# Additions of the gated branch products move from VectorE to GpSimd in a two-layer hybrid decoder trunk

## What is computed

```
h = RMSNorm(x)
proj = h @ w_in                        # 4 gates of width 1024, and the inputs of the four branches
o_a, o_b, o_c, o_d = gMLP, block-sparse attention, latent attention, convolution    # 256 tokens x 256 each
y = sum over n of sigmoid(gate_n) * (o_n @ w_branch[n])       # 256 x 1024
x = x + y @ w_out
x = x + channel_mixer(RMSNorm(x))
```

## Time and profile before

| | |
|---|---|
| device time, median of 3 | 1124.6 us |
| device time of the profiled execution | 1124.35 us |
| its span | 1122.6 us |
| TensorE busy | 1064.7 us (95%), 5632 matmuls |
| VectorE busy | 838.5 us (75%) |
| ScalarE busy | 646.7 us (58%) |
| GpSimd busy | 29.0 us (3%) |
| chain that ended last | TensorE 74%, VectorE 18%, ScalarE 5% |
| mixer of layer 0, mixer of layer 1 | about 17 to 232 us, about 436 to 650 us |

### The profile page before, as it was taken

The page is one execution under the profiler, slowest core; times in us unless marked ns, Lnnn a source line. Parts: engine busy times, 40 slices in busy tenths (PEclk is TensorE's granted clock), DMA queues, the critical chain, the costliest instruction groups (busy, mean ns, idle before and its releaser), DMA issues.

```text
span 1122.6 us, 15778 instructions
## 1 busy us (share of the span) xinstructions
PE 1064.7 (95%) x5632; PEld 910.9 (81%) x5632; DVE 838.5 (75%) x1178; ACT 646.7 (58%) x904; POOL 29.0 (3%) x76
## 2 busy tenths in 40 slices
PE   5999999999999999999899969999999999999997
PEld 4888777889999998888687857888787878788886
DVE  4579888654545447579898565988889898989895
ACT  4667545443434336456545345666767676667664
POOL 6000000030000000000000000000000000000000
PEclk9999989999999999999999988999999999999999
DMA  9554445675455454444345374899898989898981
GB/s 264 178 169 150 150 132 180 210 205 187 152 187 174 169 195 156 152 160 160 125 155 198 119 258 146 292 326 334 297 342 290 357 286 357 289 350 300 353 296 58
DMA packets 125324, 248.64 MB, mean 221 GB/s; under 512 B 4912, under 2 KB 50034, under 8 KB 125280
## 3 DMA queue, kind: packets, MB, share of 16 engines
q1 hardware_dynamic: 123136, 243.02, 63.4%
q0 software_dynamic: 2144, 5.03, 1.9%
HBM read 246.99 MB, written 1.05 MB: 221 GB/s over the span
## 4 chain that ended last, share of the span: by engine, by line
PE 74%; DVE 18%; ACT 5%; issue 2%; DMA 1%; ACTq 0%; DVEq 0%; POOL 0%; POOLq 0%
PE bank L349 22%; PE bank L351 21%; PE bank L350 21%; DVE wlo L337 8%; ACT whi L330 3%; PE bank L899 2%; PE bank L898 2%; PE bank L957 1%; DVE h L1355 1%; DVE dacc L1560 1%; PE bank L612 1%; DVE x L1353 1%; DVE h L1492 1%; DMA gain<-in_attn_norm 1%; PE bank L919 1%
## 5 line engine op out<-in xcount | busy, mean ns | idle before, releaser
L337 DVE TENSOR_TENSOR wlo<-ring,whi 128x1024 fp32r<-128x1024 f32 (+3 forms) x506 | 541.1, 1120 | 108.3 <-ACT whi L330 107.4
L349 PE MATMUL bank<-whi,hTh 128*128 128x512 f32 (+3 forms) x1328 | 479.3, 361 | 11.4 <-DVE wlo L337 8.8
L330 ACT CAST whi<-ring 128x1024 fp32r<-128x1024 f32 (+3 forms) x506 | 457.1, 972 | 30.1 <-PE bank L351 17.6
L351 PE MATMUL bank<-whi,hTl 128*128 128x512 f32 (+3 forms) x1328 | 469.2, 353 | 0.0
L350 PE MATMUL bank<-wlo,hTh 128*128 128x512 f32 (+3 forms) x1328 | 469.1, 353 | 0.0
L349 PEld LDWEIGHTS bank<-whi,hTh 128*128 128x128 f32 x1328 | 252.4, 190 | 51.6 <-DVE wlo L337 15.7
L351 PEld LDWEIGHTS bank<-whi,hTl 128*128 128x128 f32 x1328 | 252.2, 190 | 30.6
L350 PEld LDWEIGHTS bank<-wlo,hTh 128*128 128x128 f32 x1328 | 252.5, 190 | 28.3 <-issue 0.5
L349 PE MATMUL bank<-whi,oTh 128*128 128x512 f32 x128 | 53.2, 415 | 4.0 <-DVE oTl L1666 4.0
L1678 DVE SCALAR_TENSOR_TENSOR act<-bank,rstd,sig 128x256 f32<-128x256 f32 x22 | 9.6, 479 | 57.9 <-ACT sig L1209 57.9
L350 PE MATMUL bank<-wlo,oTh 128*128 128x512 f32 x128 | 51.7, 404 | 0.0
(11 more groups left out here) (299 smaller groups left out, 877.7 us busy)
## 6 DMA issues: line engine op xcount, KB each, us to landing
ring<-in_w_in SPq DMA_DIRECT2D x40, 1024.0 KB, 5.2
ring<-in_moe_w_down SPq DMA_DIRECT2D x40, 1024.0 KB, 6.0
ring<-in_moe_w_gate SPq DMA_DIRECT2D x32, 1024.0 KB, 7.2
ring<-in_moe_w_up SPq DMA_DIRECT2D x32, 1024.0 KB, 7.3
ring<-in_moe_w_gate SPq DMA_DIRECT2D x16, 768.0 KB, 6.1
ring<-in_moe_w_up SPq DMA_DIRECT2D x16, 768.0 KB, 4.5
ring<-in_ffn_w_gate SPq DMA_DIRECT2D x11, 1024.0 KB, 5.3
ring<-in_ffn_w_up SPq DMA_DIRECT2D x11, 1024.0 KB, 5.4
```

The source lines that it names most:

```text
L330: nc.scalar.copy(whi[pc.part(hf)][:, 0:n], pc.raw[:, hf * n:(hf + 1) * n]).then_inc(hi_done, 1)
L337: nc.vector.tensor_tensor(wlo[q][:, 0:n], pc.raw[:, hf * n:(hf + 1) * n], whi[q][:, 0:n].bitcast(F32), ALU.subtract).then_inc(lo_done, 1)
L349: nc.tensor.matmul(o, sh, wh, start=start, stop=False)
L351: return nc.tensor.matmul(o, sl, wh, start=False, stop=stop)
```

## The change

The products stay on VectorE and now count on a semaphore of their own, `br_used`. The additions of the steps j = 2 to 7 are done by GpSimd in `merged_sums(l)`, two for each step, and they count on `br_ev`. For j = 0 and 1, where there is nothing to add, VectorE waits for its two products and raises `br_ev` by 2 with an empty instruction. `branch(j)` on TensorE waits for the products alone; `gate_ev` and `merged_T` still wait for `br_ev`, now for GpSimd's additions.

```diff
-        br_ev = sem("br_ev")
+        br_ev, br_used = sem("br_ev"), sem("br_used")
...
+            def merged_sums(l):
+                for j in range(2, STEPS):
+                    c = j % 2
+                    pool.wait_ge(br_ev, 2 * STEPS * l + 2 * j - 2)
+                    for m in range(MT):
+                        pool.wait_ge(br_used, 2 * STEPS * l + 2 * j + m + 1)
+                        y = ym[:, m, 512 * c:512 * (c + 1)]
+                        nc.gpsimd.tensor_tensor(y, y, gsig[:, c, m, :], ALU.add).then_inc(br_ev, 1)
+
             load_gain(1)
+            merged_sums(0)
             pool.wait_ge(layer_done, 1)
             load_params(1)
             load_gain(2)
             load_gain(3)
+            merged_sums(1)
...
                     if j == 0:
                         pe.wait_ge(prj_ev, n_chunk * l + 5)
                     else:
-                        pe.wait_ge(br_ev, 2 * STEPS * l + 2 * j)
+                        pe.wait_ge(br_used, 2 * STEPS * l + 2 * j)
...
                 for m in range(MT):
                     y = ym[:, m, 512 * c:512 * (c + 1)]
                     g = gsig[:, j % 2, m, :]
-                    if i == 0:
-                        V.tensor_tensor(y, g, bank[m][:, :], ALU.mult).then_inc(br_ev, 1)
-                    else:
-                        V.tensor_tensor(g, g, bank[m][:, :], ALU.mult).then_inc(dve_seq, 1)
-                        own[0] += 1
-                if i:
-                    for m in range(MT):
-                        y = ym[:, m, 512 * c:512 * (c + 1)]
-                        dve.wait_ge(dve_seq, own[0] + m + 1 - MT)
-                        V.tensor_tensor(y, y, gsig[:, j % 2, m, :], ALU.add).then_inc(br_ev, 1)
+                    V.tensor_tensor(g if i else y, g, bank[m][:, :], ALU.mult).then_inc(br_used, 1)
+                if i == 0:
+                    dve.wait_ge(br_used, 2 * STEPS * l + 2 * j + 2)
+                    V.engine_nop().then_inc(br_ev, 2)
```

## The result

The changed kernel takes 1131.07 us (median of 4 runs, 1129.31 to 1132.16) against 1124.68 us for the kernel before in runs beside it: the ratio is 1.0057 with a 95% interval of 1.0044 to 1.0070, so it is 6.4 us slower. The profiled execution, 1132.16 us with a span of 1130.4 us, is the slowest of the four, 7.8 us over that of before. The kernels of the experiments differ by a few lines again. A VectorE instruction is called held where it lasts longer than the same instruction does in the kernel before, because GpSimd is reading.

The account below looks back on a forecast made before the run. TensorE, busy 95% of the span, was taken to bound the kernel, VectorE mattering only where TensorE waits. 1.2 + 2.2 (the two chains) + 1.7 (clock) = +5.1 us on 1124.35 gave 1129.5 us, own range 1126 to 1133.5, 8-in-10 range 1117 to 1133.5.

Parts of the forecast that it names:

- the clock: TensorE's low clock: no change behind the first wait, +1.7 us behind the longer second wait in layer 0 (bounds 0 and +3.4).
- The exclusion: GpSimd reading SBUF and VectorE instructions with two SBUF inputs lock each other out; full exclusion as forecast, chance 0.52.
- The other reading of the select: GpSimd's select L508, 0.89 us instead of 0.30, is slow through its two-term pattern, not through VectorE's split.
- One addition's hold: Each GpSimd addition of 128x512 behind a merge takes 1.1 us, holding VectorE's split for that time.
- A merge's net cost: Merges 2 to 7 on VectorE: 1.8 us of waiting less 1.2 us of additions removed, +0.6 us each.
- chain A: VectorE's work from the scores through merge 2 to L1503, before TensorE's transposes L612: +0.6 us, in two layers +1.2.
- chain B: From L1570 through merge 5 to L1666, before TensorE's `branch(6)`: +1.1 us with merges 3 and 4's delay, two layers +2.2.
- The empty instruction: With the wait for j = 0, 1: some 0.2 us of VectorE four times, covered by idle time; put at nothing.
- The transposes: TensorE's transposes in `merged_T(1)`, waiting for step 7's additions: 0, with 0.1 us to spare; otherwise +1 us each layer.
- no exclusion: Rival: GpSimd's additions don't hold VectorE, whose chains lose 4.8 us; 1116.8 us, chance 0.23.
- half exclusion: Rival: reads take turns or part of an addition holds VectorE, 0.8 us each; -2 to +2 us, 1124.5 us, chance 0.17.
- The late additions: Rival: GpSimd's addition takes 2 us or waits for two splits, TensorE waits at L720; 1133 us and over, chance 0.08.

Follow-up runs that it names:

- pool25: The changed kernel with GpSimd adding only for steps 2 and 5, VectorE adding at once for the others; 1128.76 us, ratio 1.0036 to the kernel before.
- pool34: The changed kernel with GpSimd adding only for steps 3 and 4, VectorE adding at once for the others; 1126.58 us, ratio 1.0019 to the kernel before.
- pool67: The changed kernel with GpSimd adding only for steps 6 and 7, VectorE adding at once for the others; 1125.85 us, ratio 1.0007 to the kernel before.
- write_only: The changed kernel with GpSimd's 24 additions replaced by memsets that only write, sums left out; 1116.6 us, ratio 0.9927 to the kernel before.
- write_long: The changed kernel with each GpSimd addition replaced by three memsets, one after the other, sums left out; 1119.08 us, ratio 0.9952 to the kernel before.
- one_input: The changed kernel with GpSimd's additions replaced by copies with one SBUF input, sums left out; 1118.86 us, ratio 0.9957 to the kernel before.
- warm: The changed kernel with one more small GpSimd addition (128x128) early in the program; 1131.67 us in one run.
- vector_late: The changed kernel without GpSimd additions: VectorE adds all, steps 2 and 5 later, where it stood idle; 1117.62 us, ratio 0.9941 to the kernel before.

## Why the prediction was right

The forecast was 1129.5 us and slower, +5.1 us; measured are 1131.07 us, +6.4 us, inside its own range. The path and the sizes of the holds were as forecast; the clock was not, and in part by chance.

- Where the time counts. Two merges of each layer in the chains, two before the second chain, two with hardly any effect: `pool25`, `pool34` and `pool67` show +3.9, +1.8 and +1.0 us, the last not told from nothing.
- The exclusion. I read it from one select of 64 columns and 42 ns. `write_only`, `write_long` and `one_input` show it: with reads the splits are held, without them not. The other reading of the select is out too, as the changed kernel's own trace shows. There the select starts 0.07 us before the first split (16.34) and, with the same two-term pattern, takes 0.29 us:

```profile
16.27 0.29 POOL L508 TENSOR_SCALAR_AFFINE_SELECT before_e<-before_e 128x64 f32<-128x64 f32 x1
```

- One addition's hold: 1.1 us taken, 1.10 measured. The Trainium skill's ratio ("GPSIMD Engine Reference", section "Performance versus the Vector engine") gave an estimate of 1.18 us for the whole instruction; the trace has 1.29 us of duration, 1.10 of hold. The sum of +6.4 us that I gave with it is the measured one by luck: the hold was 1.10, and the rest came from the clock.
- A merge's net cost: +0.6 us forecast, +0.69 measured. The wait in chain A went from 4.28 to 5.0 us (4.9 forecast), that of chain B from 1.99 to 3.2 (3.1 forecast). The order, half a split between two additions, was as forecast: the holds are 0.79 and 1.10 us on the two halves. For all of TensorE's waiting the chains' terms gave +3.4 us, and its idle time grew by 2.9. The empty instruction cost chain A nothing: VectorE still waited 0.56 us for TensorE ahead of it.
- The transposes: 0 with 0.1 us to spare was slightly wrong; measured is +0.35 us in each layer. The second addition of step 7 lets the first long split go ahead, and the transposes wait for it.
- The mis-sized term is the clock. I put +1.7 us for chain B in layer 0, which came. The sums over the traces give +4.4 us up to 720 us. Behind chain A the losses went from 2.4 to 2.0 us in layer 0 and from 1.6 to 2.1 in layer 1, so my nothing there holds. The rest is 1.7 us at the beginning of mixer 1 and 1.0 in the router's stretch behind it, neither of which I had looked at. The first is not a mechanism of the change, as `warm` shows. The second is not GpSimd's doing, as `vector_late` loses the same 8.3 us in the router's stretch.

The rivals: no exclusion fell with `write_only`, which gave that rival's time only once the reads were gone, and half exclusion with the hold of 1.10 us, which is beyond its turning point of 0.8. The late additions exist, at 0.7 us in two layers, not as the rival had them.

What stays open is the clock's own part. Kernels with the same two waits spread from 1114.1 to 1121.7 us over their runs (`vector_late`), while those of before lie within 3.8 us in all groups of runs. The one trace of `vector_late`, 1114.1 us, has 9.95 us of low-clock loss by the same sum. Windows over the router in it and, second, in the kernel before:

```profile
650.00:660.00 10.00, 5.40 (x27) 3.97 (x25) 8.55 (x32) 5.65 (x7) 0.00 (x0) 0.67 0.55 188
660.00:670.00 10.00, 8.19 (x35) 7.81 (x36) 2.64 (x6) 3.05 (x4) 0.00 (x0) 0.50 0.01 2
670.00:680.00 10.00, 9.83 (x38) 7.71 (x37) 3.43 (x4) 4.83 (x7) 0.00 (x0) 0.86 0.28 105
```
```profile
660.00:670.00 10.00, 3.96 (x25) 3.24 (x22) 8.86 (x33) 5.60 (x7) 0.00 (x0) 0.66 0.55 185
670.00:680.00 10.00, 8.60 (x36) 8.12 (x37) 2.76 (x4) 3.50 (x5) 0.00 (x0) 0.50 0.01 2
680.00:690.00 10.00, 9.83 (x36) 7.59 (x35) 2.73 (x3) 4.15 (x5) 0.00 (x0) 0.81 0.31 105
```

The router's stretch runs some 10 us earlier in `vector_late`, and the low clock lasts about as long there. By the same sum it takes 8.3 us in `vector_late` (648 to 673 us) and 7.3 in the kernel before (663 to 684 us), so the router isn't where `vector_late` wins. What `vector_late` lacks are the low stretches behind the two chains. They took 5.8 us before (2.4 and 1.6 behind chain A, 1.7 behind chain B in layer 1) and nothing here, and one of 1.6 us at 17 to 21 us is new. Windows around the end of chain A in layer 0, before and in `vector_late`, with the one of `write_only`, whose wait there is the same 3.1 us:

```profile
140.00:150.00 10.00, 7.08 (x30) 5.88 (x32) 8.36 (x14) 3.81 (x6) 0.00 (x0) 0.66 0.34 105
```
```profile
138.00:148.00 10.00, 6.92 (x46) 5.24 (x45) 9.89 (x17) 5.07 (x9) 0.00 (x0) 1.00 0.32 105
```
```profile
141.00:151.00 10.00, 8.31 (x44) 6.92 (x45) 7.33 (x14) 4.63 (x8) 0.00 (x0) 0.83 0.39 112
```

So a wait of 3.1 us was followed by the low clock in one trace and not in the other. The low stretch of `write_only` costs 1.7 us. The six runs of `vector_late` are in the order of their mean granted clock: 0.988 in the two at 1114.1 and 1114.9 us, 0.987 and 0.985 in between, 0.982 at 1121.7. Of about 1060 us of busy time 0.006 is an estimate of 6.4 us, most of the spread of 7.6. The runs of the kernel before show no such order (0.980 to 0.985 within 3.8 us). Which waits are followed by the low clock, and why, no run isolates.

## What to carry to other kernels

Before work goes to GpSimd, look at what VectorE does at that moment, not at how idle GpSimd is: an addition with two SBUF inputs held the VectorE instructions with two SBUF inputs that came up (splits, a tap, L1514) for 1.10 us, where VectorE needed 0.60 for the addition itself. Beside an instruction with one SBUF input (a product with a PSUM bank, a reciprocal), or in VectorE's idle time, it cost nothing. And first ask whether the work must be done there at all: moving it behind the chain that TensorE waits for gave the whole gain without a second engine, once the consumers that needed only the products had a count of their own.

## What was not expected of the hardware

- A copy on GpSimd holds VectorE 0.41 us for 512 columns, an addition 1.10 us: 0.80 against 2.15 ns a column, so the second input costs more than the first, or the addition itself slows the reading; no run parts the two.
- When both engines have such instructions ready, they took turns one by one in the pairs behind the merges: split, addition, split. Even the select of 64 columns waited 0.6 us for a split of 880 ns and then went ahead of the next one.
- The first `tensor_tensor` of the program on GpSimd is late by about 1 us (2.44 us against 1.29); a small one in advance takes that away (0.94 us for 128 columns). The first copy of `one_input` is late by as much.
